# Gated delta rule over eight chunks: the triangular inverse on 64x64 diagonal blocks with one joining level, and the stages of three neighbouring chunks interleaved

## The reference, cut to what matters

```python
g = cumsum(g);  decay = exp(where(incl, g_i - g_j, -inf))
k_beta = k * beta
t_mat = where(strict, (k_beta @ k.T) * decay, 0) + eye
u = solve(t_mat, v * beta);  w = solve(t_mat, k_beta * exp(g))
qk = (q @ k.T) * decay;  q_dec = q * exp(g);  k_tail = k * exp(g_last - g)

def step(state, ...):            # chunk after chunk
    v_new = u - w @ state
    o     = q_dec @ state + qk @ v_new
    state = state * exp(g_last) + k_tail.T @ v_new
```

## Time and profile before

| | value |
|---|---|
| runs | 6798.16, 6800.79, 6812.05 us |
| profiled execution, span | 6812.4 us |
| granted TensorE clock, whole execution | 0.840 |
| PE busy / DVE busy / ACT busy / POOL busy | 76% / 46% / 16% / 3% |
| stage `dn`: last store copy starts, first loop matmul starts | 1063.95, 543.64 us |

### The profile page before, as it was taken

How to read it: one execution, slowest core, us unless ns; L and a number is a source line. 1 busy time by engine, 2 the same in 40 slices (tenths; PEclk the granted TensorE clock), 3 DMA queues, 4 the chain that set the end, 5 groups by cost and what they waited for, 6 DMA issues and landing times. The chain is left out here.

```text
span 6812.4 us, 88762 instructions
## 1 busy us (share of the span) xinstructions
PE 5198.9 (76%) x36228; PEld 3977.3 (58%) x36250; DVE 3153.4 (46%) x4036; ACT 1076.5 (16%) x1479; POOL 216.1 (3%) x157
## 2 busy tenths in 40 slices
PE   6797883399729898567577979768459976969988
PEld 4677882289707687234335858542435544758876
DVE  8435666544464575647474432325232345432233
ACT  3102222222212100310010210001111133111100
POOL 0000000011100000000000000003010000000000
PEclk8898996699858998568788889886558788989999
DMA  1221103511122353242323122233230012322233
GB/s 69 81 83 44 34 28 141 185 53 53 47 103 97 117 188 113 84 173 74 124 87 121 54 92 99 81 122 93 79 71 4 7 37 68 130 75 74 72 125 123
DMA packets 265766, 596.61 MB, mean 88 GB/s; under 512 B 27970, under 2 KB 126705, under 8 KB 264778
## 3 DMA queue, kind: packets, MB, share of 16 engines
q1 hardware_dynamic: 192614, 411.18, 18.2%
q10 hardware_dynamic: 55360, 120.08, 4.7%
q0 software_dynamic: 17536, 61.63, 2.6%
HBM read 400.61 MB, written 192.19 MB: 87 GB/s over the span
## 5 line engine op out<-in xcount | busy, mean ns | idle before, releaser
L386 PE MATMUL gu_ps<-kept_h_hi,gu_w_hi 128*128 128x512 f32 x704 | 275.0, 391 | 40.6 <-DVE gu_w_lo L119 40.6
L386 PE MATMUL gu_ps<-kept_h_lo,gu_w_hi 128*128 128x512 f32 x704 | 274.8, 390 | 0.0
L386 PE MATMUL gu_ps<-kept_h_hi,gu_w_lo 128*128 128x512 f32 x704 | 274.6, 390 | 0.0
L386 PE MATMUL win_ps<-kept_hn_hi,win_w_hi 128*128 128x512 f32 x576 | 224.9, 390 | 39.5 <-DVE win_w_lo L119 39.5
L3576 PE MATMUL be_ps<-be_hi,be_w_hi 128*128 128x512 f32 x512 | 202.9, 396 | 58.0 <-DVE be_lo L119 57.7
L386 PE MATMUL win_ps<-kept_hn_hi,win_w_lo 128*128 128x512 f32 x576 | 224.6, 390 | 0.0
L386 PE MATMUL win_ps<-kept_hn_lo,win_w_hi 128*128 128x512 f32 x576 | 224.6, 390 | 0.0
L3576 PE MATMUL be_ps<-be_lo,be_w_hi 128*128 128x512 f32 x512 | 200.6, 392 | 0.0
L3576 PE MATMUL be_ps<-be_hi,be_w_lo 128*128 128x512 f32 x512 | 200.6, 392 | 0.0
L2214 PE MATMUL lc_ps<-idft,lc_zz 128*128 128x256 f32 x512 | 121.0, 402 | 90.9 <-DVE lc_zz L2092 90.9
L421 DVE COPY win_o<-win_ps 128x1024 f32<-128x1024 f32 x36 | 44.1, 1225 | 285.5 <-PE win_ps L386 285.5
(11 more groups left out here) (678 smaller groups left out, 12647.1 us busy)
## 6 DMA issues: line engine op xcount, KB each, us to landing
rk_in<-s_decayed SPq DMA_DIRECT2D x8, 3072.0 KB, 16.0
oproj_mod_w<-in_ada_w POOLq DMA_DIRECT2D x12, 2048.0 KB, 9.3
gu_w<-in_w_gu SPq DMA_DIRECT2D x44, 512.0 KB, 3.3
win_w<-in_w_in SPq DMA_DIRECT2D x36, 512.0 KB, 3.3
s_z<-win_o ACTq DMA_DIRECT2D x36, 512.0 KB, 2.6
s_decayed<-rkp_ring SPq DMA_DIRECT2D x32, 512.0 KB, 2.8
dn_kv<-s_qkv SPq DMA_DIRECT2D x16, 768.0 KB, 6.0
oproj_w<-in_odd_w SPq DMA_DIRECT2D x24, 512.0 KB, 4.3
```

Source lines behind the costliest of these rows:

```text
L386: mm = pe.matmul(ps[:, u, h, :], a, b, start=(k == 0 and n == 0), stop=(k == kt - 1 and n == len(pairs) - 1))
```

## The change

`delta_net` is written anew; class `Inverse` goes. What the new one does:

- **Inverse.** `LV` is 6: levels 0 to 5 work on the two 64x64 diagonal blocks only. Tiles `x`, `xt`, `ys`, `at` and `off` have 64 columns per head, upper block in partitions 0 to 63, lower in 64 to 127. `blocks` issues one matmul of 64x64 for each of both halves, one behind the other. A level's additions change only the half of the columns that can change (`half`). Level 6, the joining one, is `level_y(6)` and `level_z(6)`: two products of 64x64 per head between the blocks (`at6`, from `corner`). The whole inverse is put together in `xtf`, whose fourth quarter stays zero.
- **Three chunks in one turn.** The turns are unrolled and run from i=-1 to 8. A turn holds chunk i's inverse, chunk i+1's preparation (`sums`, `key_products`, `query_products`, `turn_keys`, `turn_values`) and chunk i-1's recurrence (`read_state`, `solve`, `outputs`, `add_state`). Their pieces stand between `level_y` and `level_z` of each level. Tiles that live over turns are double (`turns`, `kv`, `ends`, `at6`).
- **PSUM.** Per direction: `level` and `joined` for the inverse, `first` for the preparation, `second` for the recurrence, the beta rows and the turned keys.
- **GpSimd** takes `kbd`, `qd`, the fading of the state (`sd`), all masks (`off`, three levels per instruction), the `ends` copies and six memsets. VectorE's minimum with 0 and multiplication with `tri` become one minimum with `cap` (0 or -1e30). The `now` copies go.
- **Loads.** The masks are those of the 64-wide blocks; the gates' inputs are loaded before the constants.

```diff
-    LV = 7
+    LV = 6
+    XN = 2 * LV + 1
...
+                def blocks(out, a, b, which=(0, 1)):
+                    for h in range(NH):
+                        for e in which:
+                            mm = pe.matmul(out[block(e), h, :], a[block(e), h, :], b[block(e), h, :], start=True, stop=True)
+                    return mm
...
+                def turn_keys(d, c):
+                    s = per[d]
+                    pe.wait_ge(s["kb"], c + 1)
+                    if c >= 2:
+                        pe.wait_ge(s["s_ready"], c - 1)
...
+                def level_y(d, i, l):
...
+                    elif l < LV:
+                        pe.wait_ge(s["x_ready"], i * XN + 2 * l - 1)
+                        mm = blocks(level[d][:, 0, :, :], off[d][:, l, :, :], x[d])
...
+                def level_z(d, i, l):
...
+                    if l < LV:
+                        blocks(level[d][:, 1, :, :], xt[d], ys[d], (0, 1) if l < LV - 1 else (d,))
+                        mm = blocks(joined[d][:, 0, :, :], ys[d], xt[d])
+                    else:
+                        for h in range(NH):
+                            mm = pe.matmul(joined[d][early[d], 0, h, :], ys[d][late[d], h, :],
+                                           turns[d][i % 2]["xtf"][late[d], h, late[d]], start=True, stop=True)
...
+                def read_state(d, k):
+                    s, b = per[d], bufs[d]
+                    pe.wait_ge(s["kbd"], k + 1)
+                    pe.wait_ge(s["s_ready"], k)
+                    pe.wait_ge(s["kb"], min(k + 3, NCH))
...
+                for i in range(-1, NCH + 1):
+                    k, c = i - 1, i + 1
+                    here, ahead, behind = 0 <= i < NCH, c < NCH, k >= 0
```

More of the change, by code:

```diff
@@ L803, in _ @@
                     pool.wait_ge(stored[u], 16 * turns)
[L806 to L863, removed]
@@ L891, in delta_net @@
         lc = st.sb("lc", [P, 2, NCH, 4])
[L892 to L898, removed]
@@ L899, in delta_net @@
-        per = [{n: st.sem(f"{n}{d}") for n in names} for d in range(2)]
[L900 to L906, removed]
-            def _(sp):
[L908 to L913, removed]
+        level = [st.ps(f"level{d}", [P, 2, NH, RH]) for d in range(2)]
@@ new lines, in delta_net @@
+        joined = [st.ps(f"joined{d}", [P, 2, NH, RH]) for d in range(2)]
+        first = [st.ps(f"first{d}", [P, NH, P]) for d in range(2)]
+        second = [st.ps(f"second{d}", [P, NH, P]) for d in range(2)]
+        const_in, gate, gate_act, gate_t, zeroed = (
+            st.sem(n) for n in ("const_in", "gate", "gate_act", "gate_t", "zeroed"))
+        names = ("kv_in0", "kv_in1", "cum", "beta", "diff", "capped", "e_decay", "decay", "kb", "kk", "at", "at6", "qk", "pt",
+                 "k_turned", "k_copied", "v_turned", "v_scaled", "ends", "kbd", "qd", "off", "y_done", "ys_copied", "z_done",
+                 "x_ready", "joint", "s_faded", "read", "rest", "v_new", "v_copied", "v_tail", "out", "o_copied", "stored",
+                 "state_add", "s_ready")
@@ new lines, in delta_net, with chunk, half @@
+        at6 = [[st.sb(f"at6{d}{u}", [P, NH, RH]) for u in range(2)] for d in range(2)]
+        off = [st.sb(f"off{d}", [P, LV, NH, RH]) for d in range(2)]
+        kv = [[st.sb(f"kv{d}{u}", [P, 12, P]) for u in range(2)] for d in range(2)]
+        last = [P - 1, 0]
+        block = lambda e: slice(RH * e, RH * e + RH)
+        early, late = [block(0), block(1)], [block(1), block(0)]
+        def chunk(d, c):
+            return c if d == 0 else NCH - 1 - c
+        def half(t, l, s):
+            return t.rearrange("p h (b s e) -> p h s b e", s=2, e=1 << l)[:, :, s]
@@ L3382, in constants @@
     c["tri"] = np.stack([j <= i, j >= i], 1).astype(f)
-    c["masks"] = level_masks().transpose(2, 0, 1, 3)
+    c["cap"] = np.where(c["tri"] > 0, 0, NEG)
     same = (i // RH) == (j // RH)
```

635 lines of the change are left out of this document (443 added, 192 removed).

## The result

The changed kernel takes 6602.59 us (median of five runs, 6590.39 to 6649.54), the kernel before 6812.05 (five runs, 6798.16 to 6852.69): ratio 0.9693, 95% interval 0.966 to 0.9725, so faster by some 3.1%. The forecast was 6602, in a range of 6565 to 6655.

What follows compares the result with a forecast made beforehand. TensorE was taken as the bound, by issue, then the inverse's chain. Stage 14 + 30.3 + 6 x 39.8 + 30.2 + 9.5 = 322.8 against 521.0 us; with 1 us ahead, 6800.8 - 199.2 = 6601.6, rounded 6602; range 6565 to 6655.

Steps and rivals of the forecast that it cites:

- Issue, 34.3 us: TensorE's matmuls and transposes in a full turn, mostly full products and alternating quarters: 34.3 us against 49.8 before.
- Switches, 16 x 0.16: TensorE going between 64x64 and 128x128 shapes 16 times a turn: 2.6 us, bounds 0 and 3.2.
- Rival 1: Switches fall partly where TensorE waits anyway: full turn 36.5 us, total 6579 us; chance 0.22.
- Waits, 2.9 us: TensorE's waits in a full turn, for `kb`, second directions' `x`, level 6 and `new_state`: 2.9 us.
- rival 2: The chain binds: one late result holds all three chunks in TensorE's queue; turn 48 us, total 6664 us; chance 0.17.
- The turn, 39.8 us: A full turn as TensorE's issue, shape switches and waits: 34.3 + 2.6 + 2.9 = 39.8 us.
- Clock 1.00 from turn 0 on: Sign to check in the trace: TensorE's granted clock at 1.00 from turn 0, else the clock stays low.
- The ends: Partial turns: turn -1 14 us, turn 0 30.3, turn 7 30.2, turn 8 9.5; ahead of the loop 1 us less.
- Other engines: Busy time in a full turn: VectorE 22 us, ScalarE 11 to 12, GpSimd 15; none near the turn's length.
- Rival 3: VectorE and GpSimd block each other on SBUF operations: up to 23 us on the path, 6625 us; chance 0.06 in full.
- Rival 4: TensorE's clock stays at the level of 0.55: turn 68 us, total 6829 us, slower than before; chance 0.03.
- Rival 5: No interleaving, each piece waits for its own turn's inverse: turn about 55 us, stage 432, total 6711 us; chance 0.02.

Runs made afterwards that it cites:

- double_quarters: Changed kernel with every quarter matmul of levels 0 to 5 issued twice: 6714.07 us, stage 433.4 us, ratio 0.9865 to the kernel before.
- extra_drains: Changed kernel with a pair of quarter matmuls put inside each of the four groups of `sums` in a turn: 6617.91 us, stage 333.2 us.
- late_keys: Changed kernel with `turn_keys` moved behind level 6's `z`, next to `turn_values`: 6597.49 us, stage 317.1 us.
- kb_first: `late_keys` with `kb` of each direction directly behind its `cap` on VectorE: 6589.72 us, stage 315.1 us.
- filled: `tuned` with `turn_values` between level 6's `y` and `z`, and `turn_keys` last: 6605.88 us, stage 311.6 us.
- tuned: `late_keys` with `kb` directly behind its `cap`, and both directions' level 5 `x` ahead of the `xtf` pieces: 6605.99 us, stage 321.6 us.
- vector_masks: Changed kernel with the mask products moved from GpSimd to VectorE: 6623.08 us, stage 352.1 us.
- one_chunk: Changed kernel without interleaving: preparation, inverse and recurrence of one chunk per turn, one after the other, on every engine: 6625.67 us, stage 354.7 us.
- after_again: The changed kernel timed once more, code identical: 6624.05 us, stage 333.4 us.

## Why the prediction was right, point by point

- **Issue, 34.3 us.** Right. The pair pace is 0.058 (0.47 per sixteen records). The unpaired matmuls, the one term without a row, were taken at 0.11: level 6's second `y` (L1277, eight records) lasts 0.65 us, its last record 0.22, so 0.43 over seven steps, 0.12 per matmul. Where they meet a paired group they overlap with it: level 5's `z` took 1.63 us (704.83 to 706.46) where 16 paired and 8 unpaired matmuls at these paces give 1.81. `double_quarters` shows that issue is what bounds.
- **Switches, 16 x 0.16.** Right: 0.15 and 0.21 in the trace, 0.17 isolated. That each change of shape costs time agrees with what the Trainium skill says ("TensorEngine Tiling (Array Packing)", Key Properties: a change of tiling mode drains TensorE); the trace shows the price and not the drain itself. Rival 1 (hidden, turn 36.5) is refuted by the turn of 40.03 us at full clock, and `extra_drains` shows switches that are paid in full; what it adds ahead of `kb` hides that wait of 0.34 us and no more.
- **Waits, 2.9 us.** Right in place and nearly in size: `new_state` 0.97 (1.0), level 6's second `y` 0.54 (0.45), `kb` 0.34 (0.6), the second direction's `y` about 0.18 a level (682.54 to 683.81 is 1.27 for 0.93 of issue and a switch; 0.2). Two of my own signs did not hold: `kb` was to be near 1 us (my walk had 0.6), and the wait on `x` passed the 0.5 us that was to speak for rival 2, with a turn nowhere near rival 2's.
- **The turn, 39.8 us.** At clock 1.00 it is 40.03. The mean is 41.0. **This is the step that was mis-sized:** "Clock 1.00 from turn 0 on" failed. I charged the wait on `new_state` its length alone; four full turns of six fell to 0.95 to 0.97 behind it, 1.1 to 1.9 us each, 6 us in the stage. In `late_keys`, `kb_first` and `filled`, which take the wait away, no full turn is slow; `tuned` takes it away too and has the low clock behind another stall, and `extra_drains` keeps it and has one slow turn of six. So a stall at the turn's end goes before the low clock in these full turns, but which stalls bring it is not shown. I had the evidence: in the earlier trace rows the clock falls to 0.60 and 0.55 after TensorE stood still.
- **The ends.** Turn -1 14.0 (14), turn 0 30.4 (30.3), turn 7 29.5 (30.2), turn 8 9.0 (9.5), ahead of the loop 1.5 us less (1), from the copy into `dn_lc` to the first matmul (1.54 us before, 0.06 now).
- **The sum.** 329.0 against 322.8. Saved in the stage 192.0 (198.2). That the median came within 1 us of the forecast is luck beyond this. The medians before and after differ by 209.5 us, more than the stage saved, since the five runs before have their median at 6812.05 and not at the 6800.8 that I started from, and the unchanged `nsa` alone moves an execution by up to 50 us. The range was said to take in most of rival 2, whose own figure, 6664, lies outside it.
- **Other engines.** VectorE 20.6 us a turn (22), the strided additions of 128 columns 0.288 (0.28); ScalarE 10.8 (11 to 12); GpSimd 14.8 (15).
- **Rival 2** (the chain binds, 48 us): not here; `vector_masks` shows how near it is: 3.7 us more on VectorE (24.3 against 20.6) made the turn 3.6 us longer, 1.9 of them more wait on `dn_s` (2.83 us against 0.97), the rest with its full turns at clock 0.91 to 0.96. **Rival 3** (blocking): it is there, but in turn 0 alone. `cap` took 748 ns on average, but 692 in the median and 1587 once; the first `xt` 515, 416 and 1839 once. Both long ones (561.08 and 563.56) stand beside GpSimd's masks of turn 0 (from 560.84 to 564.60); in the full turns the masks come later than these two, and `cap` takes 0.69 us each time. In `vector_masks`, without GpSimd's masks, the longest `cap` is 694 ns and the longest first `xt` 420. That is 2.5 us of VectorE's time in the whole stage, not 23 on the path. It depends on the order: in `one_chunk` all sixteen first `xt` are long. **Rival 4** (low clock throughout): 0.97, refuted. **Rival 5** (no interleaving): `one_chunk` is what it would look like, 354.7 us, not the 432 that I had priced (a turn of 44.7, not 55); even then most of the gain would have come. That is the reasoning's weak point: I credited the interleaving with hiding some 15 us a turn, and without it a turn is only 3.0 to 3.7 us longer. Most of the waits of before were gone with the quarters, the smaller additions and the masks on GpSimd. No run separates these three.

## What to carry to other kernels

Price a smaller tile by its issue pace and add a price for each change of shape (here 0.17 us), and read both from a stage that has them already; the order of the engines' queues comes after. A wait on TensorE costs its length and may cost as much again in clock (here 1.1 to 1.9 us behind waits of 0.54 and 0.97): move the one operation that waits for a late result behind work that waits for nothing, and put work with no wait in front. Look at the longest single duration and not only at the mean when two engines may block each other. Judge a variant by its stage's length in the trace, at equal granted clock, when another stage moves the total by more.

## What the runs showed of the hardware that I had not expected

- The `nsa` stage, the same code in all kernels, took 413 to 467 us with a mean granted clock of 0.83 to 0.72, and the profile names no cause; what sets it stays open.
- TensorE's clock fell to 0.64 over 4 us at two waits of 0.54 and 0.97 us, and to its lower level (0.50) behind a wait of 2.8 us. With the same two waits it fell in four of six full turns in the changed kernel, in six in `after_again` and in one in `extra_drains`. In `tuned` it fell to 0.63 where the profile names no wait above 0.2 us, behind a joining product that took 1.51 us for 0.9 of issue.
- VectorE's first `xt` (both inputs in SBUF) takes 0.42 us alone and 1.15 to 1.54 us beside a GpSimd product, and ends 0.3 us after that product does.
- Matmuls in one quarter run at 0.12 us alone, 0.058 in alternation, and overlap across the boundary of two groups.
